# Three small unused buffers in the on-chip memory of a seven-stage transformer kernel, so that wide buffers begin at other addresses

## What is computed

```python
def first_block(x, ...):
    for i in range(2):
        h = rwkv7_time_mix(x, ...) if i == 0 else moba_attention(x, ...)
        x = layer_norm(ALPHA * x + h, ...)
        x = layer_norm(ALPHA * x + swiglu_ffn(x, w_in, w_down), ...)
    return x

def second_block(x, mem, ...):
    z = rmsnorm(x, ln1) @ w_in
    ...
    x = x + concatenate([ml_out, fx_out]) @ w_out
    x = x + cross_attention(rmsnorm(x, ln_x), rmsnorm(mem, ln_mem), w_xq, w_xkv, w_xo)
    ...
```

## The kernel before

| buffer | begins | bytes | start mod 128 |
|---|---|---|---|
| w_raw, w_hi, w_lo | 16512, 41088, 65664 | 24576 each | 0 |
| x_tm, mix_hi, mix_lo | 90240, 98432, 106624 | 8192 each | 0 |
| base_c, par | 114816, 116864 | 2048, 912 | 0 |
| stats, mv, sd, rstd, shift, square, eps_c, mx, sm | 117792 to 118112 | 96, 16, 8, 8, 8, 16, 12, 32, 32 | 32 to 96 |
| rs | 118144 | 32, ends at 118176 | 0 |
| ar (recurrent stage) | 118176 | 16384 | 32 |
| v_tm, rw_c | 134656, 142848 | 8192, 5384 | 0 |
| lora_wa, sw, av, kk | 148256 and on | 1024, 8192 x3 | 32 |
| sig_hi, sig_b | 173856, 174880 | 1024 each, end at 175904 | 32 |
| rx_hi, rx_lo, xt, less_mu, mixed | 175904 and on | 8192 x4, 16384 | 32 |
| laid over these: dd_a, dd_b, nt_m, w_m, rb, akrk_b, ... cum to kmod, u_m, sa_m | 175904 and on | 512 to 8192 | 32 |
| x_hi, x_lo, xn, x_fm, gain, xk_fm (all later stages, over ar and on) | 118176, 126368, 134560, 142752, 150944, 159136 | 8192 x5, 8288 | 32 |
| gsel, sel, gate_w, gate_bf, gate_bi | 167424 to 174176 | 6144, 48, 512, 4, 4 | 0, 0, 64, 64, 96 |
| hid, act_f, hid_hi, hid_lo | 174208 and on | 4096 each | 0 |
| laid over these: ma_q to rope_c; conv_out, ml_v, ..., bias; xq_fm, cr_s, cr_p, cr_o | 174208 and on | 1024 to 8192 | 0 |
| se_o (the last of the highest group) | 227040 | 2048, ends at 229088 | 96 |

## Time and profile before

### The profile page before, as it was taken

How to read it: one execution, slowest core, us unless ns; L and a number is a source line. 1 busy time by engine, 2 the same in 40 slices (tenths; PEclk the granted TensorE clock), 3 DMA queues, 4 the chain that set the end, 5 groups by cost and what they waited for, 6 DMA issues and landing times.

```text
span 1177.8 us, 24790 instructions
## 1 busy us (share of the span) xinstructions
PE 1142.7 (97%) x10562; PEld 1044.4 (89%) x10562; DVE 747.2 (63%) x1081; ACT 623.3 (53%) x913; POOL 108.9 (9%) x89
## 2 busy tenths in 40 slices
PE   6999899999999999999999999999999999999997
PEld 6798777789999989998999999899998898999996
DVE  7888775474644467897645444768487555555554
ACT  8974654464344345575634433666556565544443
POOL 0032263501100000220010000000000000000000
PEclk9999999999999999999999999999999999999999
DMA  8631111046444644423555447264533443655650
GB/s 303 221 106 52 52 55 49 22 162 239 179 174 183 249 180 151 172 109 144 179 215 185 182 169 252 106 215 180 179 108 137 173 156 107 233 182 179 211 178 36
DMA packets 29804, 187.30 MB, mean 159 GB/s; under 512 B 3472, under 2 KB 5648, under 8 KB 8592
## 3 DMA queue, kind: packets, MB, share of 16 engines
q1 hardware_dynamic: 27072, 177.21, 41.7%
q10 hardware_dynamic: 2640, 8.75, 2.3%
HBM read 184.90 MB, written 1.05 MB: 158 GB/s over the span
## 4 chain that ended last, share of the span: by engine, by line
PE 85%; DVE 8%; ACT 4%; issue 2%; DMA 0%; ACTq 0%; DVEq 0%; SPq 0%
PE ps L2095 25%; PE ps L2096 24%; PE ps L2097 24%; PE ps L2562 1%; PE ps L2416 1%; PE ps L2421 1%; ACT mixed L631 1%; DVE w_lo L1365 1%; PE ps L2228 1%; PE ps L2418 1%; PE ps L2358 1%; PE ps L2804 1%; PE ps L2812 1%; DVE x_tm L1618 1%; DVE stats L1621 1%
## 5 line engine op out<-in xcount | busy, mean ns | idle before, releaser
L1369 DVE TENSOR_TENSOR w_lo<-w_raw,w_hi 128x2048 fp32r<-128x2048 f32 x149 | 346.9, 2345 | 131.0 <-ACT w_hi L602 130.5
L2095 PE MATMUL ps<-x_hi,w_hi 128*128 128x256 f32 x1344 | 378.2, 281 | 4.3 <-DVE x_lo L1656 2.4
L2096 PE MATMUL ps<-x_lo,w_hi 128*128 128x256 f32 x1344 | 374.9, 279 | 0.0
L2097 PE MATMUL ps<-x_hi,w_lo 128*128 128x256 f32 x1344 | 374.8, 279 | 0.0
L602 ACT CAST w_hi<-w_raw 128x2048 fp32r<-128x2048 f32 x148 | 281.8, 1907 | 147.7 <-PE ps L2097 147.1
L2095 PEld LDWEIGHTS ps<-x_hi,w_hi 128*128 128x128 f32 x1344 | 252.6, 188 | 10.6 <-issue 5.6
L2096 PEld LDWEIGHTS ps<-x_lo,w_hi 128*128 128x128 f32 x1344 | 252.7, 188 | 1.3
L2097 PEld LDWEIGHTS ps<-x_hi,w_lo 128*128 128x128 f32 x1344 | 252.7, 188 | 0.0
L2095 PE MATMUL ps<-w_hi,hid_hi 128*128 128x512 f32 x304 | 118.8, 391 | 0.1
L2096 PE MATMUL ps<-w_lo,hid_hi 128*128 128x512 f32 x304 | 118.7, 390 | 0.0
L2097 PE MATMUL ps<-w_hi,hid_lo 128*128 128x512 f32 x304 | 118.3, 389 | 0.0
(11 more groups left out here) (402 smaller groups left out, 1774.6 us busy)
## 6 DMA issues: line engine op xcount, KB each, us to landing
w_raw<-in_weights SPq DMA_DIRECT2D x163, 1024.0 KB, 4.9
xt<-in_xT SPq DMA_DIRECT2D x2, 512.0 KB, 5.5
w_raw<-in_weights SPq DMA_DIRECT2D x2, 512.0 KB, 6.3
x_tm<-in_x SPq DMA_DIRECT2D x1, 1024.0 KB, 7.5
gain<-in_mix_g ACTq DMA_DIRECT2D x2, 512.0 KB, 4.4
gain<-in_mix_b ACTq DMA_DIRECT2D x2, 512.0 KB, 6.5
gain<-in_ffn_g ACTq DMA_DIRECT2D x2, 512.0 KB, 7.4
gain<-in_ffn_b ACTq DMA_DIRECT2D x2, 512.0 KB, 8.2
```

What stands on the lines that cost most here:

```text
L1369: V.tensor_tensor(w_lo[:, i % WS, :], w_raw[:, i % RAW, :], w_hi[:, i % WS, :].bitcast(F32), ALU.subtract).then_inc(lo_done, 1)
L2095: nc.tensor.matmul(out, hi_l, hi_r, start=start, stop=False)
L2096: nc.tensor.matmul(out, hi_l, lo_r, start=False, stop=False)
L2097: return nc.tensor.matmul(out, lo_l, hi_r, start=False, stop=stop)
```

## The change

Three buffers are reserved that no instruction names: 27 elements per partition (108 bytes) after rs, 6 elements (24 bytes) after sig_b inside the recurrent stage's group, 26 elements (104 bytes) after gate_bi. What is reserved after each begins further on. No instruction, wait, transfer or shape is edited.

```diff
         mx = sb("mx", [P, 8])
         sm = sb("sm", [P, 8])
         rs = sb("rs", [P, 8])
+        sb("to_line_a", [P, 27])
         ident = base_c[:, 0:P]
...
             sig_hi = sb("sig_hi", [P, T], F32R, a_rw)
             sig_b = sb("sig_b", [GB, T], F32R, a_rw)
+            sb("to_line_b", [P, 6], where=a_rw)
             with ExitStack() as a:
                 rx_hi = sb("rx_hi", [P, KT, T], F32R, a)
...
         gate_w = sb("gate_w", [P, KT, 16], where=a_m)
         gate_bf = sb("gate_bf", [12, 1], where=a_m)
         gate_bi = sb("gate_bi", [36, 1], where=a_m)
+        sb("to_line_c", [P, 26], where=a_m)
```

## The result

The changed kernel takes 1187.32 us (median of 8 runs, 1184.57 to 1189.01) against 1180.86 for the kernel before measured beside it: a ratio of 1.0058, interval 1.0046 to 1.0069. That is 6.5 us slower, where no change was forecast, and outside the range given. The profiled execution took 1185.86 us, its span is 1184.1, 6.3 us longer than before.

What follows compares the result with a forecast made beforehand. The prediction took TensorE, busy 97% of the span, to bound the kernel. Its terms for TensorE, VectorE with ScalarE, and loads summed 0 + 0 + 0 on the 1181.05 us median: 1181.0 us, range 1178.3 to 1183.7.

Steps and rivals of the forecast that it cites:

- The addresses: Buffer starts, rounded to 32 bytes: x stays 32 past a multiple of 128; only the overlay goes from 32 to 64 past.
- As x keeps its offset, the term is 0: TensorE's 4704 products with x_hi and x_lo: no change, since x stays 32 bytes past a multiple of 128.
- The comparison of rows: TensorE products with x (32 past) against mix (0 past): 281 and 279 against 282 and 281 ns, difference 0 to 1 ns.
- The bound: TensorE products with x, if their offset did change: one rounding step, 1 ns x 4704 = 4.7 us, either side.
- VectorE and ScalarE, 0 of at most 1.9 us: 622 instructions up to 232 us: taken as 0, bounded by 3 ns each, 1.9 us gain or loss.
- loads, 0 of at most 0.8: First loads, chiefly xt moving from 32 to 64 past: taken as 0, with 0.8 us kept both ways.
- The signs of being wrong: Wrong if products with x shift 1 ns or more throughout, or the 130 to 232 us stretch changes over 2 us.
- TensorE gains with the address: Rival on the 4704 TensorE products with x: 1 ns less each, 4.7 us faster, 1176.3 us; chance 0.05.
- exact packing: Buffers placed by exact size without 32-byte rounding, so the gaps would bring wide buffers to multiples of 128.
- the overlay collides: Rival in the first 232 us, mainly the recurrent stage: 10 ns x 622 = 6.2 us slower, 1187.2; chance 0.06.
- The rule on 16-byte lines: On-chip memory accesses: each line crossing costs, but all starts stay multiples of 16, so the term is 0.

Runs made afterwards that it cites:

- e4: A 128-byte gap ahead of w_raw, so every buffer begins 128 bytes further on, against the kernel before: ratio 1.0000.
- e3: No gaps; sel, gate_bf and gate_bi reserved ahead of x_hi, moving only x and its neighbours by 128 bytes, against the kernel before: ratio 1.0060.
- e2: Second and third gap without the first: overlay 32 bytes and hid 128 further on, x unmoved, against the kernel before: ratio 1.0032.
- e9: A 128-byte gap between w_hi and w_lo, moving w_lo and all behind it, against the kernel before: 1184.49 us, ratio 1.0041.
- e10: x moved 160 bytes and hid 256 further on, against the kernel before: 1178.37 us, ratio 0.9990; its repeat 0.9981.
- e11: x moved 160 bytes and hid 192 further on, against the kernel before: 1173.07 us, ratio 0.9932; its repeat 1170.41 us, 0.9927.

## Why the prediction was wrong

- **The addresses** were worked out rightly: x stays 32 past a multiple of 128, and only the overlay changes there. The step that failed came after: "the large buffers keep their position within 128 bytes" was taken to mean that nothing changes for TensorE ("As x keeps its offset, the term is 0"). Two things were wrong in it. What counts is a distance between buffers, not an offset (e4). And it repeats every 256 bytes as far as hid shows (227.8 ns at 0, 227.7 at 256, 233.0 at 128), so a shift by 128 isn't a whole turn. x moved by half a turn against weights that stayed, and in place of 0 the term was 1.7 and 1.65 ns a product, 8.0 us by the sum of the steps and 6.5 in the measured time.
- **The comparison of rows** could have warned me. I took "w_lo,x_hi" for products that stream x; they stream w. Read rightly, hold x streamed at r = 32 (279 ns in "x_lo,w_hi", no wait before it), w streamed beside x at r = 224 (281) and w streamed beside mix at r = 0 (282 and 281). The 2 ns between the first two are of the size of the effect itself. I put them together as "0 to 1 ns".
- **The bound** of 1 ns x 4704 = 4.7 us on TensorE was both excluded from the forecast's range and too small: the runs gave 1.7 and 1.65 ns, 8.0 us. A mean printed in whole ns bounds nothing below 1 ns, but nor does a pair of rows bound an offset that neither has.
- **VectorE and ScalarE, 0 of at most 1.9 us; loads, 0 of at most 0.8:** not contradicted, by the rows above.
- **The signs of being wrong** were half good. Products with x shifted by 1 to 2 ns throughout, and that sign caught the miss. The other could not speak: a stretch cut at 130 and 232 us is 102 us long in any trace. TensorE is busy for 93.39 us in it, against 93.35.
- **The rival "TensorE gains with the address"** had the right place and the wrong sign. It tied the effect to exact packing and gave it 0.05.
- **The rival "the overlay collides"** came to 1187.2 us, 0.1 from the measured median, and is false. Its price was a guess at 10 ns x 622, its place the first 232 us; e3 has the whole loss without touching the overlay, and e2 puts it at 64 past at no cost beyond hid's. A number that fits says nothing for a mechanism.
- **The rule on 16-byte lines** gave 0. The rows of VectorE and ScalarE agree; TensorE's don't. The same page of the Trainium skill, "SBUF — State Buffer", Who interferes with whom, gives TensorE two independent read ports and says that it never waits on anyone. The runs here speak against that independence: the step moved by some 6 ns in 120 with the distance between the two buffers that it reads.

## What to carry to other kernels

In a kernel that TensorE bounds, any new or resized buffer may change its pace, through the distance between what is streamed and what is loaded; in these runs by up to 1.4% of the time. So a change that only moves buffers should be measured and not reasoned away. Compare the mean of the same products in whole stretches without a stall, ask of each row which buffer is streamed, and undo moves one buffer at a time. Before giving the credit or the blame for a change of 1% to an edit, look whether it also moved addresses.

## What the runs showed of the hardware that I had not expected

- Steps of back-to-back products of 256 columns range from 113.6 to 120.0 ns at a full granted clock, by where the buffers begin and by something that differs between stages and executions. For 512 columns it is 226.8 to 233.9 ns. A period of 256 bytes is shown for hid (moved by 256 with no loss); for x it rests on the agreement of the two kinds.
- Products of 512 columns beside hid are good only at r = 0 (226.8 to 227.8 ns), fair at 64 (228.9 and 229.3) and 5 to 6 ns slower at 32, 128, 160, 192 and 224; r = 96 was not tried. In e9, with only w_hi at r = 128, one of its two products was slower by 3.6 ns and the other by 1.6.
- At r = 64 and r = 192 there are two paces, about 113.6 and 117.8 ns, that can last for whole stages and, at 192, differ between executions of one program. What picks the pace is open. So is where hid's place comes in, since e10 and e11 differ in that alone.
